# Scanning an RWKV-7 state by single heads instead of by block-diagonal pairs, on one Trainium2 core

## What is computed

```python
def wkv7_step(state, inp):                      # 16 heads, each state 64x64 [value, key]
    r_t, w_t, k_t, v_t, a_t, b_t = inp
    sa = jnp.einsum('bhij,bhj->bhi', state, a_t)
    state = (state * w_t[:, :, None, :] + sa[..., None] * b_t[:, :, None, :]
             + v_t[..., None] * k_t[:, :, None, :])
    y = jnp.einsum('bhij,bhj->bhi', state, r_t)
    return state, y
...
    state, y = lax.scan(wkv7_step, wkv_prev.astype(f32), xs)
    y = jnp.moveaxis(y, 0, 1)
    mu = jnp.mean(y, axis=-1, keepdims=True)
    var = jnp.mean(jnp.square(y - mu), axis=-1, keepdims=True)
    y = ((y - mu) * lax.rsqrt(var + LNX_EPS) * lnx_g + lnx_b)
```

## Time and profile before

| | us |
|---|---|
| median of 3 runs (lowest, highest) | 3002.27 (2998.17, 3007.76) |
| the profiled execution | 2994.69 |
| its span | 2992.9 |
| PE, PEld busy | 2689.9, 2531.1 |
| DVE, ACT, POOL busy | 1277.1, 944.0, 590.9 |

### The profile page before, as it was taken

How to read it: one execution, slowest core, us unless ns; L and a number is a source line. 1 busy time by engine, 2 the same in 40 slices (tenths; PEclk the granted TensorE clock), 3 DMA queues, 4 the chain that set the end, 5 groups by cost and what they waited for, 6 DMA issues and landing times. The chain is left out here.

```text
span 2992.9 us, 46796 instructions
## 1 busy us (share of the span) xinstructions
PE 2689.9 (90%) x19528; PEld 2531.1 (85%) x19528; DVE 1277.1 (43%) x2250; ACT 944.0 (32%) x1809; POOL 590.9 (20%) x357
## 2 busy tenths in 40 slices
PE   4879878958886899999999999898899999999998
PEld 3648768947775789999999999777799999999998
DVE  5236776338886742121121235466563222121223
ACT  4337623312213442121120234356543122131221
POOL 1011111113344002112112230210201222221230
PEclk7989989989997899999999999999999999999999
DMA  8866659684465412222222231411111111111121
GB/s 317 305 225 205 207 183 272 202 183 106 101 139 192 130 50 86 92 71 85 92 85 85 71 97 53 121 28 47 55 60 36 50 44 49 50 43 50 49 65 57
DMA packets 379486, 331.87 MB, mean 111 GB/s; under 512 B 109863, under 2 KB 349163, under 8 KB 372221
## 3 DMA queue, kind: packets, MB, share of 16 engines
q1 hardware_dynamic: 349180, 287.17, 32.1%
q10 hardware_dynamic: 24384, 21.87, 2.5%
q0 software_dynamic: 5728, 20.06, 1.8%
HBM read 248.92 MB, written 78.78 MB: 109 GB/s over the span
## 5 line engine op out<-in xcount | busy, mean ns | idle before, releaser
L524 POOL TENSOR_TENSOR wL<-raw,wH 128x1024 fp32r<-128x1024 f32 x120 | 288.1, 2401 | 1297.0 <-ACT wH L648 1297.0
L545 PE MATMUL t_acc<-oneH,wH 128*128 128x344 f32 x1488 | 482.6, 324 | 12.3 <-DVE oneL L892 6.3
L547 PE MATMUL t_acc<-oneH,wL 128*128 128x344 f32 x1488 | 477.6, 321 | 0.0
L546 PE MATMUL t_acc<-oneL,wH 128*128 128x344 f32 x1488 | 477.2, 321 | 0.0
L545 PE MATMUL t_acc<-twoH,wH 128*128 128x344 f32 x1392 | 449.0, 323 | 7.0 <-DVE twoL L867 4.8
L547 PE MATMUL t_acc<-twoH,wL 128*128 128x344 f32 x1392 | 445.5, 320 | 0.0
L546 PE MATMUL t_acc<-twoL,wH 128*128 128x344 f32 x1392 | 445.1, 320 | 0.0
L817 DVE SCALAR_TENSOR_TENSOR X<-t_acc,mod,X 128x344 f32<-128x344 f32 (+1 forms) x240 | 137.4, 572 | 611.4 <-PE t_acc L547 590.2
L897 DVE TENSOR_TENSOR t_g<-t_g 128x344 f32<-128x344 f32 x192 | 99.3, 517 | 553.3 <-ACT t_g L668 553.3
L545 PEld LDWEIGHTS t_acc<-oneH,wH 128*128 128x128 f32 x1488 | 281.4, 189 | 26.4 <-issue 10.1
L648 ACT ACTIVATE wH<-raw 128x1024 fp32r<-128x1024 f32 x120 | 126.7, 1056 | 507.6 <-PE t_acc L547 507.6
(11 more groups left out here) (481 smaller groups left out, 5039.4 us busy)
## 6 DMA issues: line engine op xcount, KB each, us to landing
raw<-in_mlp_down SPq DMA_DIRECT2D x64, 512.0 KB, 3.8
raw<-in_mlp_up SPq DMA_DIRECT2D x62, 512.0 KB, 4.2
ada_ring<-in_ada_w SPq DMA_DIRECT2D x24, 1024.0 KB, 8.7
shared<-in_ada_w SPq DMA_DIRECT2D x24, 1024.0 KB, 6.2
kvrb_hx<-hx_saved ACTq DMA_DIRECT2D x16, 516.5 KB, 3.7
kvr_work<-scr_L SPq DMA_DIRECT2D x16, 516.0 KB, 5.1
X<-x_saved SPq DMA_DIRECT2D x6, 1376.0 KB, 7.5
raw<-in_at_wqkv SPq DMA_DIRECT2D x12, 512.0 KB, 4.0
```

The lines of the kernel that those rows point to most:

```text
L524: pool.tensor_tensor(low, raw_of(w), high.bitcast(F32), ALU.subtract).then_inc(s_low, 1)
L545: pe.matmul(out, high[:, k, :], h[:, k, third[t]], start=(k == 0), stop=False)
L546: pe.matmul(out, high[:, k, :], l[:, k, third[t]], start=False, stop=False)
L547: return pe.matmul(out, low[:, k, :], h[:, k, third[t]], start=False, stop=(k == DB - 1))
```

## The change

The scan works head by head on 64x64 tiles, with no zeros beside them.

- S and U are [128, DB, 64]: head h of block b on partitions 64h to 64h+63. B and K are kept by head, B's and K's 64 tokens side by side (BK, 128 columns for each head). V and SA of a head are stacked on the 128 partitions of one tile W, V on one half and SA on the other.
- `mm` names a row group and a column group of 64 each. U from S, SA, the product of the eye with S, and `values_in` (the masked K·A product with V) are passes of 16 products 64x64 with 64 columns streamed; Y from S (`outer`) is such a pass in two parts of eight.
- `grams`: 16 products for each chunk, 64 rows by 128 columns with 128 streamed, B and K against At and Rt at once; no decay diagonal.
- `by_token` is new: 16 products per chunk, 64 rows by 128 columns with 64 columns of an identity streamed, which turn B and K to tokens (pK). ACT copies them to Gd in two pieces.
- pD takes the old state by a product with the identity, then one product per head with Gd and the stacked W. DVE writes S = pD * decay in two pieces. POOL's Sd and diagonal are gone.
- Y's token part is one product per head with the masks' result Gm and W.
- U leaves PSUM by one ACT copy; SA by one ACT copy of 64 partitions and one DVE copy of the other 64.
- `values_in` and `by_token` for the next chunk stand at the end of a chunk, after `turn`; the pass U of a chunk then is the product with S alone.
- DVE's order in a chunk: inverse, variance, masks of half 0, SA copy, samples part 0, S, masks of half 1, mean, samples parts 1 and 2.
- SP issues B and K before the rest; ACT issues all loads of the samples first; the memsets of the block-diagonal tiles are gone.

The diff, cut to its core:

```diff
-        ARI = sb("ARI", [128, 2, DB, 3, 2, C])
-        BK = sb("BK", [128, 2, 2, 2, DB, 128])
+        AR = sb("AR", [128, 2, DB, 2, 2, C])
+        BK = sb("BK", [128, 2, DB, 2, 2 * C])
         Z = sb("Z", [128, 2, 2, DB, C])
-        V = sb("V", [128, 2, 2, DB, 128])
-        G = sb("G", [128, 2, DB, 5, C])
-        S, U, SA = sb("S", [128, DB, 128]), sb("U", [128, DB, 128]), sb("SA", [128, DB, 128])
-        Sd = sb("Sd", [128, DB, 128])
+        W = sb("W", [128, 2, 2, 2, DB, HD])
+        Gm = sb("Gm", [128, 2, 2, DB, 2, C])
+        Gd = sb("Gd", [128, 2, 2, DB, HD])
+        S, U = sb("S", [128, DB, HD]), sb("U", [128, DB, HD])
...
-                if not last:
-                    diagonal(c + 1, (k + 1) % BODY)
-                pool.tensor_tensor(Sd[:], S[:], decay.to_broadcast([128, DB, 128]), ALU.mult).then_inc(s_dS, 1)
                 normalise(c, k)
...
+            both = [(b, h) for b in range(DB) for h in range(2)]
+            def mm(out, lhsT, rhs, k, m, start, stop):
+                return pe.matmul(out, lhsT, rhs, start=start, stop=stop, skip_group_check=True, tile_position=(64 * k, 64 * m))
...
-                for q in range(4):
-                    b = 4 * half + q
-                    pe.matmul(pB[:, q, :], BK[:, s, cc, 0, b, :], ARI[:, s, b, 1:3, cc, :], start=True, stop=True, skip_group_check=True)
-                    ins = pe.matmul(pK[:, q // 2, (q % 2) * 192:(q % 2) * 192 + 192], BK[:, s, cc, 1, b, :], ARI[:, s, b, :, cc, :], start=True, stop=True, skip_group_check=True)
+                for b, h in both[8 * half:8 * half + 8]:
+                    if half == 0 and b == 2 and h == 0:
+                        inner_free(c - 1)
+                    ins = mm(pG[h][:, b - 4 * half, :], BK[at(h), s, b, cc, :], AR[at(h), s, b, :, cc, :], h, 0, True, True)
                 ins.then_inc(s_G, 1)
+            def inner_free(c):
...
+                pe.wait_ge(s_RS, c + 1)
+                pe.wait_ge(s_yTe, c + 1)
+                pe.wait_ge(s_Uev, c + 1)
+            def by_token(c, k):
+                s, cc = k // 2, k % 2
+                for b, h in both:
+                    if b == 4 and h == 0:
+                        pe.wait_ge(s_UV, c + 1)
+                        pe.wait_ge(s_Yev, c + 1)
+                        pe.wait_ge(s_S, c * 2 + 2)
+                    ins = mm(pK[h][:, b, :], BK[at(h), s, b, cc, :], eye[at(h)], h, 0, True, True)
+                ins.then_inc(s_K, 1)
+            def values_in(k):
+                s, cc, g = k // 2, k % 2, k % 2
+                for b, h in both:
+                    ins = mm(pU[at(h), b, :], Gm[at(1 - h), g, h, b, 0, :], W[at(1 - h), s, cc, h, b, :], 1 - h, h, b == 0, False)
+                ins.then_inc(s_UV, 1)
...
+                for b, h in both:
+                    ins = mm(pU[at(h), b, :], AR[at(h), s, b, 0, cc, :], S[at(h), b, :], h, h, False, True)
                 ins.then_inc(s_U, 1)
+                outer(True).then_inc(s_RS, 1)
...
+                    grams(*ahead, 0)
+                for b, h in both:
+                    ins = mm(pSA[at(h), b, :], Z[at(h), s, cc, b, :], U[at(h), b, :], h, h, True, True)
                 ins.then_inc(s_SA, 1)
+                outer(False)
+                for b, h in both:
+                    mm(pD[at(h), b, :], eye[at(h)], S[at(h), b, :], h, h, b == 0, False)
+                pe.wait_ge(s_Kev, c * 2 + 2)
+                pe.wait_ge(s_Sa, c + 1)
+                pe.wait_ge(s_Sd, c + 1)
+                for b, h in both:
+                    ins = mm(pD[at(h), b, :], Gd[:, g, h, b, :], W[:, s, cc, h, b, :], 0, h, False, True)
                 ins.then_inc(s_D, 1)
                 if not last:
                     grams(*ahead, 1)
+                for q in range(Q):
+                    for h in range(2):
+                        for b in (2 * q, 2 * q + 1):
+                            ins = mm(pY[at(b % 2), b - b % 2 + h, :], Gm[:, g, h, b, 1, :], W[:, s, cc, h, b, :], 0, b % 2, False, True)
+                ins.then_inc(s_Y, 1)
+                turn(c, k, last)
+                if not last:
+                    values_in((k + 1) % BODY)
+                    by_token(c + 1, (k + 1) % BODY)
...
                 for q in range(Q):
+                    if q == Q - 1 and not last:
+                        pe.wait_ge(s_Gev, c * 4 + 10)
                     ins = pe.transpose(pT[:, q, :], Y[:, (k - Y_LAG) % BODY, q, :], ident)
...
+                act.activation(U[:], pU[:], ACT.Copy).then_inc(s_Uev, 1)
+                act.wait_ge(s_K, c + 1)
+                for h in range(2):
+                    act.activation(Gd[:, g, h], pK[h][:], ACT.Copy).then_inc(s_Kev, 1)
                 act.wait_ge(s_SA, c + 1)
+                act.activation(W[at(0), s, cc, 0], pSA[at(0)], ACT.Copy).then_inc(s_Sa, 1)
...
+                for h in range(2):
+                    dve.tensor_tensor(Gm[:, g, h, b].rearrange("p b i t -> p b (i t)"), pG[h][:], mask, ALU.mult).then_inc(s_Gev, 1)
...
                 inverse(c)
+                dve.wait_ge(s_yi, c + 1)
+                variance(c)
                 if not last:
                     dve.wait_ge(s_Y, c + Y0)
                     masked(c + 1, 1 - g, 0)
                 dve.wait_ge(s_SA, c + 1)
+                dve.tensor_copy(W[at(1), s, cc, 1], pSA[at(1)]).then_inc(s_Sd, 1)
...
+                smp.step(dve, c, 0)
+                dve.wait_ge(s_D, c + 1)
+                for half in range(2):
+                    b = slice(4 * half, 4 * half + 4)
+                    dve.tensor_tensor(S[:, b], pD[:, b], net.pend[:, b, bass.ds(c, 1)].to_broadcast([128, 4, HD]), ALU.mult).then_inc(s_S, 1)
                 if not last:
                     masked(c + 1, 1 - g, 1)
+                mean(c, k, c)
+                smp.step(dve, c, 1)
+                smp.step(dve, c, 2)
```

## The result

| | before | after |
|---|---|---|
| median (lowest, highest), us | 3000.55 (2995.86, 3007.76), 5 runs | 2976.66 (2973.24, 2985.46), 5 runs |
| the profiled execution, its span | 2994.69, 2992.9 | 2985.46, 2983.7 |
| ratio, 95% interval | | 0.9925 [0.9902, 0.9947] |

The change gains 23.9 us (0.75%). 2952 was forecast, a gain of about 50: the sign and the range hold, but the gain is under half of that.

What follows compares the result with a forecast made beforehand. PE and DVE were taken to share the scan's bound. At 12.9 us a chunk, savings of 37.5 us plus 11 at the start and 2 at the end made 50.5: 2944 us profiled, 2952 median, range 2938 to 2978.

Steps and rivals of the forecast that it cites:

- The streams: PE's products in a chunk: six small passes at 0.94 us, outer, grams, by_token at 1.75 and turn, 10.5 us in all.
- The changes of form: Nine changes of PE's array form per chunk at 0.2 us each, 1.8 us, bringing PE to 12.3 us.
- the reading that spares changes between equal column groups: Alternative rule for PE's array: changes of form between equal column groups cost nothing, making PE's sum about 11.5 us.
- DVE's loop: The scan's loop through DVE, from SA copy to SA copy, sets the chunk period at 12.9 us; PE idles 0.6.
- The collision of POOL and DVE: Samples' parts 1 and 2 behind mean wait on POOL's subtraction and square; without this DVE would be 1.8 us shorter.
- The code: Rival: PE's scan loop code doesn't stay loaded with 1.8 times the instructions; a few us, no chance of its own.
- The loads: SP's 15 scan loads still land about 16 us behind the Y freeing the buffer, leaving 2 us of cover.
- the loads bind: Rival: scan loads land 4 us later, taking the cover and then 1 us a chunk; 13.9 us, 2967 us, chance 0.07.
- PEclk: Sign of failure: PE's clock falls to 1.2 GHz, doubling the 10.5 us of streams; 40% of the scan eats the gain.
- Start and end: Around the scan's loop: earlier samples' states gain 11 us (4 to 13) at the start; the end takes 23, not 25.0.
- the longer PE: Rival: PE bounds the scan, by_token at 2.6 us and form changes at 0.3; 14.2 us a chunk, 2972 us, chance 0.18.
- PE alone: Rival: POOL and DVE don't meet, so PE sets the scan's chunk at 12.3 us; 2941 us, chance 0.12.

Runs made afterwards that it cites:

- x12_early_small_mean: Kernel after with PE's chunks written out, two passes in fewer PE records, loads issued as buffers free, DVE's mean moved behind variance: 2921.87 us.
- x2_unroll: Kernel after with PE's sixteen chunks written out instead of looped: 2960.55 us, ratio 0.9877.
- x9_before_padded: Kernel before with 48 idle 32x32 products added per chunk, making PE's loop body 2115 records long: 3018.27 us, ratio 1.0067.
- x1_order: Kernel after with SP's load issues back in the old order, A, R and Z ahead of B and K: 2978.77 us, ratio 0.9933.
- x7_early_unroll: Kernel after with PE's chunks written out and each part of a load issued once its own buffer is free: 2941.14 us, ratio 0.9806.
- x5_early_small: Kernel after with PE's chunks written out, by_token and the eye with S in fewer records, loads issued as buffers free: 2939.7 us, ratio 0.9801.
- x4_small: Kernel after, still looped, with by_token as eight transposes and the eye with S as one 512-column product: 2969.35 us, ratio 0.9904.

## Where the prediction was right and where it failed

**The streams: right.** A small pass was put at 0.94 us and takes 0.93 (1.15 less the last record's 0.22) to 0.98 from start to start; half of the grams 0.88, with its change 1.09; by_token 1.75, and 1.93 with the change behind it. That the zeros of the old pass cost nothing, so that the products gain in the grams alone, was right too.

**The changes of form: too dear.** 1.8 us were counted. PE waits 0.21 us a chunk for DVE's SA: its step from the eye with S to D is 0.36 us, and 0.15 in the chunks behind a stall, where SA is there in time. A chunk of PE is then 11.68 us, the streams by the terms above are 10.54, and 1.14 is left, 0.13 for each change: PE's sum was 12.3 instead of 11.7. The trace prices a single change too. From the last 64x64 record to the first 64x128 one it is 0.148 us from start to start, against 0.030 inside the pass, and so over all nine: each costs 0.12 to 0.15 us. The Trainium skill ("TensorEngine Tiling (Array Packing)", Tiling Modes, Key Properties) has TensorE drain only where the tiling mode changes, not just the tile. The trace agrees: inside a pass the tile changes from record to record at 0.030 us. It doesn't bear out the reading that spares changes between equal column groups, though its sum of 11.5 is near: from 64x64 to 128x64 the step is 0.148 us as well.

**DVE's loop: the right engine, the wrong length.** 12.9 us were forecast, 11.89 measured. The largest part of the error is that the mean was put behind ACT's copy of the chunk's Y. Its wait (line 2740) counts from an initial increment, so that in chunk c it asks for the copy of chunk c - 1, as it did in the kernel before. The rows show it: the mean starts at 818.74, and ACT's copy of this chunk's Y is still running:

```profile
818.62 0.60 ACT L2650 ACTIVATE c_Y<-c_pY 128x512 f32<-128x512 f32 x1 [3.83 <-PE c_pY L2523]
```

From the end of the SA copy, at 815.09, the mean starts at 3.65 us, where 4.15 was counted. The samples' six instructions behind it take 4.19 us where about 4.5 were, since the first of them is over before POOL's subtraction starts, and the masks and the SA copy are 0.2 shorter. Together that is 1.0 us a chunk, 14 us over the scan, in favour of the change; counted rightly, the forecast would have been too fast by still more. DVE is busy for 92% of an undisturbed chunk, as was expected, and for 76% of U(1) to U(15) with the stalls.

**The collision of POOL and DVE: right.** 1.15 and 1.14 us, against 0.43 and 0.42. Moving the mean (x12_early_small_mean) shows its price, since the chunk falls by 0.83 us: less than the 1.44 of DVE's time, because PE becomes the bound. The Trainium skill ("SBUF — State Buffer", Who interferes with whom) has it that DVE instructions with two SBUF inputs are the ones that meet GpSimd's reads; here the trace agrees. In x12_early_small_mean the masks (one input in PSUM) and the copy of SA lie under POOL's two, and none of them is longer for it, POOL's no more than DVE's:

```profile
769.74 1.04 POOL L2514 TENSOR_TENSOR c_Y<-c_Y,c_ym 128x512 f32<-128x512 f32 x1 [0.90 <-DVE c_ym L2750]
770.86 1.04 POOL L2517 TENSOR_TENSOR c_ysq<-c_Y 128x512 f32<-128x512 f32 x1
```
```profile
770.05 1.29 DVE L2720 TENSOR_TENSOR c_Gm<-c_pG,const 128x512 f32<-128x512 f32 x2 [0.38 <-PE c_pG L2528]
771.37 0.69 DVE L2732 COPY c_W<-c_pA 64x512 f32<-64x512 f32 x1
```

**The code: the step that failed.** It stood among the rivals as "a few us, inside the others", with no term in the sum and no chance of its own. It was the larger cause: 16 us of the median by x2_unroll (13.7 in the scan, where 12.2 are stalls at the two jumps), and another part by way of the loads, which x2_unroll leaves in place. It should have been a term: the profile of before shows its instruction queue silent inside the scan from 721 us, and the change takes PE's loop from 1349 to 2374 records. What no row of before showed was how far 1349 lay from the edge; the price past it (x9_before_padded: 6.3 and 6.2 us for the jumps) could not be read there.

**The loads: the second step that failed, named but mis-sized twice.** "Their order changes, their bytes don't", so they were left at 16 us with 2 us of cover. The order didn't matter (x1_order). But a load's duration isn't its bytes alone: it is 18.9 to 20.5 us, of which some 3 go with the code fetches, and about 1 stays open between the store of Y and the order. And the shorter chunk, 11.89 instead of 12.9, took one of the 2 us of cover, so PE waits 3.1 to 3.7 us at four of the six loads. The rival "the loads bind" had the mechanism, 4 us later landing, with a chance of 0.07 and a price of 1 us a chunk (14 us). Its measured price is 19 us by x2_unroll against x7_early_unroll, the low clock behind the waits included.

**PEclk.** The prediction named a falling clock as a way to fail, but tied it to nothing. It fell behind every wait for a load and every jump back, and by the estimate above took most of the 12.8 us that the waits leave.

**Start and end.** The start was to gain 11 us, with 4 to 13 as ends. PE's last product of the stage ahead ends at 624.9 before and 632.8 after, so each U(1) has to be taken from there: 58.9 us before, 53.5 after, 5.4 gained, half of the 11 (U(1) itself starts at 686.3, not 673); x12_early_small_mean has 49.1. The states of the samples no longer end the wait. What is late next, which the step didn't name, is the first load, and then grams, values and tokens of chunk 0 one behind the other at half the clock:

```profile
660.02 2.08 PE L2523 MATMUL c_pG<-c_AR,c_BK 64*128 64x128 f32 x16 [5.01 <-DMA c_Z<-scr_T]
...
667.04 1.97 PE L2523 MATMUL c_pU<-c_W,c_Gm 64*64 64x64 f32 x32 [1.48 <-DVE c_Gm L2714]
668.94 3.68 PE L2523 MATMUL c_pK<-c_eye,c_BK 64*128 64x64 f32 x32
672.54 1.97 PE L2523 MATMUL c_pU<-c_S,c_AR 64*64 64x64 f32 x32
```

The tail behind U(15) was put at 23 us and takes 20.9, where it was 25.0.

**The account.** Forecast 50.5 us. To it the shorter chunk adds 14.1, the stalls take 38.2 from it, the start 5.6, and the tail gives 2.1: 22.9. Or by part, measured: 13.4 inside (51.6 from the shorter chunk, less the 38.2 of stalls), 5.4 at the start and 4.1 at the end, 22.9, near the 23.9 by which the medians differ. That the spans of the two profiled executions differ by only 9.2 is in stages that the change doesn't touch: the scan begins 7.9 us later, and behind it the kernel after takes 5.7 us more; x2_unroll, x5_early_small and x12_early_small_mean take -2 to +6 us against before there.

That the time lies inside the range is luck. The range's slow end was drawn for a PE with longer products and changes, which didn't come; what filled it was two causes of other kinds, against a chunk that was 1.0 us shorter than forecast. In the rivals three sums are off by 1 to 2 us (14.1 us a chunk for the longer PE, 2966 for the loads, 2943 for PE alone); none changes the argument.

## What to carry to other kernels

When a change multiplies the instructions in a loop, read the instruction queue of the profile before: if it is silent inside the loop, its code stays loaded, and the longer one may not. Write such a loop out or shorten it, and give the loads cover again, since each microsecond that a chunk becomes shorter is taken from the time that the next loads have. And order an engine's instructions by what runs beside them: the same nine instructions cost 1.4 us less a few places away from POOL's.

## What the runs showed of the hardware

- PE's loop code is kept between rounds at 1349 and 1426 instruction records and not at 1942, 2115 or 2374. Past that it comes in 16 KB pieces, 18 for eight chunks of x2_unroll, which at 587 records a chunk is one for every 261. Straight code hides the fetch but for 0.5 to 1.8 us in the whole scan; a jump back leaves PE idle for 4.9 to 8.3 us, in one or two parts (x4_small 4.9 and 5.0, after 6.6 and 5.6, x9_before_padded 6.3 and 6.2, x1_order 8.3 twice).
- A code fetch also slows data loads running beside it: 15.7 to 15.9 us become 16.7 with one piece, 17.1 to 18.0 with two, 18.7 to 18.9 with four and 19.5 to 20.4 with five, for the same 15 DMAs.
- In the kernel after, a stall of 3.1 to 3.7 us on PE is followed by 3.4 to 6.8 us at 1.2 GHz, and two close behind each other by 10.2 (4.2 and 2.4 us) and 6.8 (2.9 and 2.7).
- A change of the array's form costs PE 0.12 to 0.15 us in each of the chunk's nine places; a change of the tile alone costs nothing that shows.
- A 64x64 fp32 record takes 30 ns through a whole scan (31 steps in 0.93 us), near the 29 of the earlier trace rows. A record that loads 128 columns and streams 64 takes 56 ns (by_token's 31 steps in 1.73 us), and the grams' records, which load 128 and stream 128, take 59 (15 steps in 0.89): halving the stream hardly shortens the record, so here the load sets the pace.
